# Expert stage of a retention, short-conv and mixture-of-experts layer: interleaving half of the small context matmuls with the latent ones on TensorE, and moving two weight-remainder subtractions ahead of the routing hand-over

## What is computed

```python
def expert_choice_ffn(h, w_router, w_gate, w_up, w_down):
    cap = EC_CAPACITY_FACTOR * t // N_EXPERTS        # 128 latent, 16 context
    aff = jax.nn.softmax((hf @ w_router).astype(jnp.float32), axis=-1)
    vals, idx = lax.top_k(aff.T, cap)
    xs = hf[idx]
    hid = jax.nn.silu(jnp.einsum('ecd,edf->ecf', xs, w_gate)) * jnp.einsum('ecd,edf->ecf', xs, w_up)
    out = jnp.einsum('ecf,efd->ecd', hid, w_down) * vals[..., None].astype(h.dtype)
    y = jnp.zeros_like(hf).at[idx.reshape(-1)].add(out.reshape(-1, d))
```

## Time and profile before

| | before |
|---|---|
| median of 3 runs | 2237.54 us (2232.99 to 2238.55) |
| the profiled execution: time, span | 2232.99 us, 2231.2 us |
| mean granted TensorE clock | 0.966 of full |
| TensorE matmul busy | 2064.2 us, 93% of the span |
| VectorE, ScalarE busy | 1184.7 us, 739.5 us |
| expert stage | about 1413.8 to 2188 us of the span |

### The profile page before, as it was taken

How to read it: one execution, slowest core, us unless ns; L and a number is a source line. 1 busy time by engine, 2 the same in 40 slices (tenths; PEclk the granted TensorE clock), 3 DMA queues, 4 the chain that set the end, 5 groups by cost and what they waited for, 6 DMA issues and landing times.

```text
span 2231.2 us, 33423 instructions
## 1 busy us (share of the span) xinstructions
PE 2064.2 (93%) x12879; PEld 1735.5 (78%) x12879; DVE 1184.7 (53%) x1610; ACT 739.5 (33%) x848; POOL 270.1 (12%) x234
## 2 busy tenths in 40 slices
PE   5699999999999999999999892799999999999992
PEld 1488888888999999999999782577777777777771
DVE  1745545456555232322123547766777666677665
ACT  4521212221111111121112332355555555555551
POOL 1001001010000000000000121111321111231113
PEclk9799999999999999999999995899999999999996
DMA  8102111114444111112235637288876788876767
GB/s 280 50 10 78 33 52 38 43 73 124 145 139 139 38 38 47 38 47 79 80 92 199 220 130 306 88 308 304 298 264 248 296 304 303 302 282 249 273 237 271
DMA packets 182101, 364.92 MB, mean 164 GB/s; under 512 B 10404, under 2 KB 99436, under 8 KB 182052
## 3 DMA queue, kind: packets, MB, share of 16 engines
q1 hardware_dynamic: 165520, 311.23, 38.5%
q0 software_dynamic: 16432, 53.01, 8.3%
q10 hardware_dynamic: 100, 0.03, 0.0%
HBM read 321.21 MB, written 43.02 MB: 163 GB/s over the span
## 4 chain that ended last, share of the span: by engine, by line
PE 89%; DVE 5%; DMA 2%; issue 2%; ACT 1%; POOL 0%; ACTq 0%; SPq 0%; DVEq 0%; POOLq 0%
PE ps L798 10%; PE ps L800 10%; PE ps L799 10%; PE ps L1064 9%; PE ps L1066 8%; PE ps L1068 8%; PE ps L1076 8%; PE ps L820 3%; PE ps L821 3%; PE ps L822 3%; PE ps L869 2%; PE ps L870 1%; PE ps L871 1%; PE ps L979 1%; PE ps L981 1%
## 5 line engine op out<-in xcount | busy, mean ns | idle before, releaser
L1965 DVE TENSOR_TENSOR e_lo<-raw,e_hi 128x2048 fp32r<-128x2048 f32 x192 | 439.4, 2291 | 143.5 <-ACT e_hi L1422 143.4
L1422 ACT CAST e_hi<-raw 128x2048 fp32r<-128x2048 f32 x192 | 366.3, 1910 | 234.5 <-PE ps L1068 234.5
L798 PE MATMUL ps<-h_hi,w_hi 128*128 128x384 f32 x960 | 322.0, 335 | 2.3 <-DVE w_lo L1551 2.3
L799 PE MATMUL ps<-h_lo,w_hi 128*128 128x384 f32 x960 | 320.9, 334 | 0.0
L800 PE MATMUL ps<-h_hi,w_lo 128*128 128x384 f32 x960 | 320.9, 334 | 0.0
L1551 DVE TENSOR_TENSOR w_lo<-w_raw,w_hi 128x1024 fp32r<-128x1024 f32 x64 | 78.0, 1219 | 215.9 <-ACT w_hi L1185 215.8
L798 PEld LDWEIGHTS ps<-h_hi,w_hi 128*128 128x128 f32 x960 | 180.5, 188 | 9.3 <-DVE w_lo L1551 4.9
L799 PEld LDWEIGHTS ps<-h_lo,w_hi 128*128 128x128 f32 x960 | 180.5, 188 | 0.0
L800 PEld LDWEIGHTS ps<-h_hi,w_lo 128*128 128x128 f32 x960 | 180.5, 188 | 0.0
L1064 PE MATMUL ps<-e_hi,x_hi 128*128 128x512 f32 x512 | 163.2, 400 | 0.0
L1068 PE MATMUL ps<-e_hi,x_lo 128*128 128x512 f32 x512 | 161.4, 396 | 0.0
(11 more groups left out here) (267 smaller groups left out, 3439.1 us busy)
## 6 DMA issues: line engine op xcount, KB each, us to landing
raw<-in_w_gate_dram SPq DMA_DIRECT2D x64, 1024.0 KB, 8.2
raw<-in_w_up_dram SPq DMA_DIRECT2D x64, 1024.0 KB, 14.6
raw<-in_w_down_dram SPq DMA_DIRECT2D x64, 1024.0 KB, 11.4
w_raw<-in_w_in_dram SPq DMA_DIRECT2D x48, 512.0 KB, 4.1
ada_k<-in_w_ada_dram SPq DMA_DIRECT2D x64, 256.0 KB, 2.7
merged_d<-merged POOLq DMA_DIRECT2D x16, 576.0 KB, 3.5
ada<-in_w_ada_dram SPq DMA_DIRECT2D x4, 2048.0 KB, 14.0
ret_part<-merged_d POOLq DMA_DIRECT2D x8, 576.0 KB, 4.0
```

What stands on the lines that cost most here:

```text
L798: pe.matmul(out, w_hi[:, slot, k, :], xh, start=(k == 0), stop=False)
L799: pe.matmul(out, w_hi[:, slot, k, :], xl, start=False, stop=False)
L1422: act.copy(e_hi[u % 4][:].rearrange("p k n -> p (k n)"), raw[(u + 8) % 12][:].rearrange("p k n -> p (k n)"))\
L1965: dve.tensor_tensor(e_lo[u % 4][:].rearrange("p k n -> p (k n)"), raw[(u + 8) % 12][:].rearrange("p k n -> p (k n)"), e_hi[u % 4][:].rearr ...
```

## The change

Three edits. On TensorE, context 0 to 3 are no longer in the block after latent 7: each follows the latent unit of the same number, and the wait for the copied context rows moves to the head of the expert. On ScalarE, the Silu of the context's gate goes ahead of high(8) to high(11). On VectorE, low(0, 0) and low(0, 1) go ahead of the copies that follow the selection's transposes; low(0, 2) and low(0, 3) stay.

```diff
             def expert(e, last):
+                pe.wait_ge(ctx_copied, e + 1)
                 for u in range(4):
                     if u % 2 == 0:
                         pe.wait_ge(x_hi_done, 2 * e + u // 2 + 1)
                         pe.wait_ge(x_lo_done, 2 * e + u // 2 + 1)
                     latent(e, u, 0, x_hi, x_lo)
+                    context(u, 4, 0, rows_c)
                 for u in range(4, 8):
                     latent(e, u, 2, x_hi, x_lo)
-
-                pe.wait_ge(ctx_copied, e + 1)
-                for u in range(4):
-                    context(u, 4, 0, rows_c)
 
                 pe.wait_ge(out_ready, 2 * e)
                 for u in range(4, 8):
...
                     act.activation(hid[:, half * 512:half * 512 + 512], ps[:, half, :], ACT.Silu).then_inc(sg_done, 1)
-                for u in range(8, 12):
-                    high(e, u)
                 act.wait_ge(raw_used, 12 * e + 4)
                 act.wait_ge(hid_done, 3 * e)
                 act.activation(sg_c[:], ps[:, 4, 0:CAP_Q], ACT.Silu).then_inc(sg_done, 1)
+                for u in range(8, 12):
+                    high(e, u)
...
             dve.tensor_copy(sel_f[0:EXPERTS, CAP_L:CAP], sel_i[0:EXPERTS, CAP_L:CAP]).then_inc(sel_ready, 1)
+            for b in range(2):
+                dve.wait_ge(x1_stored[b], 16 * (5 - b))
+            for q in range(2):
+                low(0, q)
             dve.wait_ge(sel_turned, 1)
...
-            for b in range(2):
-                dve.wait_ge(x1_stored[b], 16 * (5 - b))
-            for q in range(4):
+            for q in (2, 3):
                 low(0, q)
             low_rows(0)
```

## The result

| | before | after |
|---|---|---|
| median | 2236.76 us (5 runs, 2232.99 to 2238.55) | 2262.17 us (5 runs, 2259.75 to 2264.11) |
| span of the profiled execution | 2231.2 us | 2260.4 us |
| expert to expert | 48.26 us | 49.61 us |
| last selection instruction to first latent matmul | 13.22 us | 17.27 us |
| ratio, 95% interval | | 1.0114, 1.0101 to 1.0129 |

The change costs 25.4 us; the sum in the prediction was 24.4.

A forecast was written before the change was run, and what follows sets the result against it. TensorE's own instruction stream was taken as the bound. Terms of 20.2 (contexts), 0.4 (copied rows) and 3.8 us (subtractions) sum to +24.4 us, giving 2257.4 or 2261.9 by base, forecast 2260, range 2250 to 2269.

The forecast's parts named there:

- TensorE's own stream bounds the stage: Expert stage: as long as TensorE's instruction stream, 48.26 us per expert; no engine or load makes TensorE wait.
- Price of contexts 0 to 3: Gate stage: four lone context units cost 4.72 us, save 3.46 in the block; +1.26 us per expert, +20.2 for 16.
- The gap belongs to the change of form: TensorE between latent and context matmuls: idle 0.36 and 0.41 us come from changing tiling form, not from the down stage.
- The wait for the copied rows: Moved to the expert's head: free for experts 1 to 15, +0.4 us for expert 0.
- Cover after latent 7: Shrunken context block still hides VectorE's `hid`, with 0.85 us to spare before the transposes; no cost.
- ScalarE's edit costs and gains nothing: The context's Silu, 0.38 us, fits ahead of high(8) without delaying it; the 1.78 us wait saved is worth nothing.
- Lows ahead of the copies: Hand-over to expert 0: two subtractions take 4.45 us, 0.68 covered; +3.8 us, or +3.4 if the second gather quickens.
- Earlier gate loads gain nothing and lose nothing: Next expert's gate loads go out one every 4 us instead of four in 2.86 us; no effect on time.
- The clock's rise at expert 0: TensorE's rise from the 1.2 GHz level may shift by a unit; 1.5 us allowed either way, nothing added.
- without a toll: Rival: moving contexts in the gate stage costs TensorE nothing; 2242 us, a change of 0.2%; chance 0.07.
- with cheaper lone units: Rival: lone context units in the gate stage cost less than in the block; -13 us, 2224 us; chance 0.04.
- with the cover gone: Rival: `hid` comes over 0.85 us later, TensorE waits 1.4 us per expert; 23 us more, 2283 us; chance 0.06.

The follow-up runs named there:

- wide_tile: Changed kernel's TensorE and ScalarE edits, every context matmul given a 128-column identity and its own accumulation group, context products left out; 2704.44 us, measured once.
- tensor_only: Kernel before plus the TensorE edit alone, contexts 0 to 3 after their latent units; 2256.81 us against 2235.57, ratio 1.0095.
- lows_four: Kernel before with low(0, 0) to low(0, 3) all ahead of the selection's copies; 2239.68 us, measured once.
- the last run: Kernel before with down-stage contexts in one block after latent 11, VectorE's first subtractions waiting until GpSimd issued expert 0's gathers; 2214.51 us, ratio 0.9909.
- silu_only: Kernel before plus ScalarE's edit alone, the context's Silu ahead of high(8) to high(11); 2389.63 us, measured once.

## Why the prediction was right

- **TensorE's own stream bounds the stage**: held. With the other two edits left out, the expert still takes 49.61 us.
- **Price of contexts 0 to 3**: expected +1.26 us per expert, measured +1.35; the mechanism was right and the size a little low. The prediction subtracted a gate-stage latent unit (2.80) from a down-stage pair (3.98). In the gate stage the pair takes 4.00, so the lone unit costs 1.20: 4 x 1.20 - 3.46 = 1.34. The term of 20.2 us thus measured 21.55.
- **The gap belongs to the change of form**: held, by wide_tile. The Trainium skill, TensorEngine Tiling (Array Packing), Key Properties, has a change of tiling mode drain TensorE. The runs agree and give the price, 0.34 to 0.41 us per passage; that the wait inside is such a drain, they do not show.
- **The wait for the copied rows**: expected +0.4 us once, measured +0.46 (tensor_only).
- **Cover after latent 7**: held; TensorE waits for `hid` nowhere in the changed kernel, and even with a single context unit there only for 0.17 us. The spare time came out as reckoned: `hid` ends at 1799.31 + 1.28 = 1800.59, 0.85 us ahead of the transposes at 1801.44.
- **ScalarE's edit costs and gains nothing**: held beside TensorE's edit.
- **Lows ahead of the copies**: expected +3.8 us (3.4 if the gathers got quicker), measured +3.66 with gathers as slow as before. The 0.4 us back did not come: nearly half of the second gather was free of subtractions, as the prediction had it, but by the rows under lows_four a gather ends a fixed time after the subtraction in which it starts, and that one was still there. No run varies this alone. Taking the plain row and not the rule was right in its result; the reason was seen only in the runs.
- **Earlier gate loads gain nothing and lose nothing**: held.
- **The clock's rise at expert 0**: allowed 1.5 us either way; about 1.1 against the one execution before. As kernels with the same code there differ as much, this is not shown to be a term of the change.
- **The absolute times of the hand-over**: forecast 1405.2 for the copy of `halves` and 1418.0 for the first latent matmul, read 1408.07 and 1420.86. Both are late by the 3.0 us that lie ahead of the last selection instruction; counted from there, the first latent matmul came 4.05 us later and 4.2 were expected.

The rivals without a toll, with cheaper lone units, and with the cover gone are all excluded by the pitch of 4.00 us and the absence of a wait for `hid`. That the forecast of 2260 lies only 2.2 us from the median is in part luck, as the five runs of the kernel before alone span 5.6 us; the sum, term by term, is 1.2 us short (25.6 against 24.4).

## What to carry to other kernels

When TensorE has no idle time to give, the order of its matmuls is a cost by itself: count how often the stream passes between full-array and column-tiled matmuls, price a passage from the starts of weight loads on a repeated pattern, and put small tiled matmuls in as few blocks as buffers and covers allow. Moving work to "earlier" helps only if someone waits for it; two subtractions that lay wholly beside the gathers became 3.7 us of pure delay ahead of them. And price two neighbouring patterns with rows of the same stage, and a wait of several microseconds with the clock that falls behind it.

## What the runs showed of the hardware

- A passage into four 32-column tiles and back cost 0.34 to 0.41 us. In the rows of the weight loads it shows as two idle times of 0.36 and 0.41 us, which together are longer than what it costs. Between plain float32 and rounded float32 matmuls of full width there was no gap (wide_tile).
- Sixteen matmuls of 256 columns in four column tiles took 0.864 us inside a block, and 3.46 us when each took the full width (wide_tile).
- Issuing an indirect gather took GpSimd 2.34 us beside VectorE's subtractions and 1.06 beside an idle VectorE; in the last run the one for expert 1, issued beside low(0, 2), took 2.64 us instead of 0.96. The first and second gathers of expert 0, before and after, end 0.74 to 0.94 us after the subtraction that was running when they started. The subtractions were not slowed in return: four took 8.90 us beside the gathers and 8.88 ahead of them. The Trainium skill, SBUF — State Buffer, SBUF: two separate sides, describes an exclusion between a VectorE instruction with two SBUF inputs and a GpSimd instruction that reads SBUF; the waiting of the gathers fits it, but the runs do not show the lock itself.
- After a wait of about 6.3 us of TensorE in silu_only the granted clock read 0.50, the 1.2 GHz level, where it had read 1.00 between 1730 and 1737; some 3.9 us of lost time came on top of the wait.
- Latent units take 2.72 us in the down stage and 2.80 in gate and up, with the same instruction forms. Why was not tried and stays open.
